# Attention units: three score tiles in flight instead of two, and the last value matmuls between the branch projections

## The reference, cut to what matters

```python
q_a, kc, vc, ks, vs, kw, vw, g_nsa, cq, ckv, kr, g_merge = split(u @ w_in)
# branch a, for each group of 4 heads and each block of 128 queries:
#   three softmaxes (over 15 compressed keys, over the selected keys, over a window), gated and summed
# branch b (latent attention), 8 heads: keys and values from the 256-wide latent, rotary part added
p = exp(s - max(s)); p = p / maximum(sum(p), 1)
y = sigmoid(g_a) * (o_a @ w_branch_a) + sigmoid(g_b) * (o_b @ w_branch_b)
return y @ w_out
```

## Time and profile before

| | |
|---|---|
| runs, median (lowest to highest) | 2415.97 us (2414.37 to 2419.86) |
| profiled execution, its own time | 2425.54 us |
| span of the profiled execution | 2423.5 us |
| mean granted TensorE clock | 0.971 of full |
| PE busy | 2314.7 us, 96% |
| DVE, ACT, POOL busy | 1581.6, 1173.8, 369.3 us |
| attention units of layer 0, of layer 1 | from 331 to 476 us, from 993 to 1138 us |

### The profile page before, as it was taken

The page is one execution under the profiler, slowest core; times in us unless marked ns, Lnnn a source line. Parts: engine busy times, 40 slices in busy tenths (PEclk is TensorE's granted clock), DMA queues, the critical chain, the costliest instruction groups (busy, mean ns, idle before and its releaser), DMA issues.

```text
span 2423.5 us, 41857 instructions
## 1 busy us (share of the span) xinstructions
PE 2314.7 (96%) x17252; PEld 2042.7 (84%) x17252; DVE 1581.6 (65%) x2225; ACT 1173.8 (48%) x2044; POOL 369.3 (15%) x360
## 2 busy tenths in 40 slices
PE   7999999799999999988999999999999998999998
PEld 7888977798888889777888998788878988878887
DVE  5886766578868867665776587267566553535753
ACT  3654444455546544434555566365456411345542
POOL 0110022111101100211111202120132440032001
PEclk9999998899999999988999999999998999999999
DMA  7877742257757766522566554345533300333553
GB/s 267 285 260 239 259 171 97 72 183 267 251 193 280 259 241 251 179 87 87 167 223 210 168 172 143 126 159 189 191 112 122 114 4 3 130 126 115 195 181 105
DMA packets 114236, 417.18 MB, mean 172 GB/s; under 512 B 12672, under 2 KB 12928, under 8 KB 113664
## 3 DMA queue, kind: packets, MB, share of 16 engines
q1 hardware_dynamic: 113184, 409.56, 49.7%
q10 hardware_dynamic: 864, 4.96, 0.5%
HBM read 413.42 MB, written 1.05 MB: 171 GB/s over the span
## 4 chain that ended last, share of the span: by engine, by line
PE 81%; DVE 8%; ACT 4%; issue 4%; POOL 2%; DMA 1%; POOLq 0%; DVEq 0%; ACTq 0%
PE banks L517 80%; DVE weight_lower L1395 2%; ACT heap L2239 1%; DVE weight_ring L1406 1%; POOL heap L2589 1%; ACT weight_upper L2120 1%; PE banks L908 0%; DVE nmax L1552 0%; DVE heap L1550 0%; DVE heap L1533 0%; ACT L2154 0%; DMA weight_ring<-ffn_up_dram 0%; DMA c_rows<-c_rows_dram 0%; PE banks L1196 0%; ACT heap L2284 0%
## 5 line engine op out<-in xcount | busy, mean ns | idle before, releaser
L517 PE MATMUL banks<-xn_halves,weight_upper 128*128 128x512 f32 (+1 forms) x3680 | 1021.0, 349 | 8.0 <-DVE weight_lower L1395 6.0
L1395 DVE TENSOR_TENSOR weight_lower<-weight_ring,weight_upper 128x1024 fp32r<-128x1024 f32 x580 | 738.2, 1279 | 329.2 <-ACT weight_upper L2120 328.0
L517 PE MATMUL banks<-xn_halves,weight_lower 128*128 128x256 f32 x2832 | 809.0, 286 | 23.1 <-DVE branch_a_lower L1587 13.0
L2120 ACT ACTIVATE weight_upper<-weight_ring 128x1024 fp32r<-128x1024 f32 x580 | 608.6, 1054 | 347.7 <-PE banks L517 228.1
L517 PEld LDWEIGHTS banks<-xn_halves,weight_upper 128*128 128x128 f32 x3680 | 650.3, 194 | 99.3 <-DVE weight_lower L1395 6.4
L517 PEld LDWEIGHTS banks<-xn_halves,weight_lower 128*128 128x128 f32 x2832 | 545.5, 193 | 32.3 <-DVE branch_a_lower L1587 15.1
L517 PE MATMUL banks<-hidden,weight_upper 128*128 128x512 f32 x1216 | 428.7, 398 | 4.9 <-DVE heap L1474 4.2
L517 PE MATMUL banks<-hidden,weight_lower 128*128 128x256 f32 x1216 | 340.5, 280 | 0.0
L517 PEld LDWEIGHTS banks<-hidden,weight_upper 128*128 128x128 f32 x1216 | 228.4, 188 | 62.0 <-DVE heap L1474 5.2
L2589 POOL TENSOR_TENSOR heap<-heap 128x256 f32<-128x256 f32 x120 | 121.4, 1016 | 962.6 <-ACT heap L2336 634.9
L517 PEld LDWEIGHTS banks<-hidden,weight_lower 128*128 128x128 f32 x1216 | 229.4, 189 | 0.0
(11 more groups left out here) (287 smaller groups left out, 2610.9 us busy)
## 6 DMA issues: line engine op xcount, KB each, us to landing
weight_ring<-w_ada_dram SPq DMA_DIRECT2D x144, 512.0 KB, 4.4
weight_ring<-ffn_gate_dram SPq DMA_DIRECT2D x88, 512.0 KB, 3.6
weight_ring<-ffn_up_dram SPq DMA_DIRECT2D x88, 512.0 KB, 3.6
weight_ring<-ffn_down_dram SPq DMA_DIRECT2D x88, 512.0 KB, 3.5
weight_ring<-m_w_up_dram SPq DMA_DIRECT2D x64, 512.0 KB, 3.9
weight_ring<-m_w_down_dram SPq DMA_DIRECT2D x64, 512.0 KB, 4.2
weight_ring<-w_in_dram SPq DMA_DIRECT2D x58, 512.0 KB, 4.3
weight_ring<-b_w_rkv_dram SPq DMA_DIRECT2D x24, 512.0 KB, 3.6
```

Of the source, the lines that this page charges most:

```text
L517: return nc.tensor.matmul(o, w, r, start=first, stop=last)
L1395: V.tensor_tensor(w_lo[:, n % RING, :], ring[:, n % RING, :], w_hi[:, j % SPLITS, :].bitcast(F32), ALU.subtract).then_inc(*did("weight_low ...
L2120: A.activation(w_hi[:, j % SPLITS, :], ring[:, n % RING, :], ACT.Copy).then_inc(*did("weight_upper", j))
```

## The change

The scores of unit u lie in place u % 3; the third place is the buffer `latent_n`, whose last reader (the matmuls that make the latent keys, values and queries) stands ahead of the units. `nmax` and `den` get three places too. The banks stay two pairs. PE now computes the scores of units 0 and 1 ahead of the first merge, of unit 2 between merges 1 and 2, and in round u those of unit u+3 instead of u+2. DVE and ACT follow: DVE does `back(u)`, `front(u+3)`, `scale(u+2)` in a round (it was `scale(u+1)`, `back(u)`, `front(u+2)`), ACT does `exps(u+2)` (it was `exps(u+1)`) and then, as before, the merge copy and `back(u)`. The values of the last output run between `w_a` and `w_b` of the first chunk, and their `out_lower` on DVE behind the gating of `w_a`. On ACT the two sigmoids move ahead of the last outputs.

```diff
-        nmax = sb("nmax", [P, 2, HPG])
-        den = sb("den", [P, 2, HPG])
+        nmax = sb("nmax", [P, 3, HPG])
+        den = sb("den", [P, 3, HPG])
+        def scores_of(u):
+            return scores[:, u % 3] if u % 3 < 2 else latent_n[:, 0:HPG, :]
...
-                for m in range(MERGES_FIRST):
-                    merge(m)
                 unit_scores(0)
                 unit_scores(1)
+                merge(0)
+                merge(1)
+                unit_scores(2)
+                for m in range(2, MERGES_FIRST):
+                    merge(m)
...
-                    if u + 2 < NU:
-                        unit_scores(u + 2)
+                    if u + 3 < NU:
+                        unit_scores(u + 3)
...
-                unit_values(todo.pop())
...
+                        if c == 0 and name == "w_b":
+                            unit_values(todo.pop())
...
                 front(0)
                 front(1)
                 scale(0)
+                front(2)
+                scale(1)
                 todo = []
                 for u in range(NU):
-                    if u + 1 < NU:
-                        scale(u + 1)
                     back(u)
+                    if u + 3 < NU:
+                        front(u + 3)
                     if u + 2 < NU:
-                        front(u + 2)
+                        scale(u + 2)
...
-                out_lower(todo.pop())
...
+                        if c == 0 and name == "w_b":
+                            out_lower(todo.pop())
...
-                    if u + 1 < NU:
-                        exps(u + 1)
+                    if u + 2 < NU:
+                        exps(u + 2)
...
+                    if u >= NU - 2:
+                        e = u - (NU - 2)
+                        act.wait_ge(*due("merge", (l, MERGE - 1)))
+                        a = gm[:, e * KD:(e + 1) * KD, :]
+                        A.activation(a, a, ACT.Sigmoid).then_inc(*did("merge_gate", (l, e)))
                 out_t(todo.pop())
-                for e in range(2):
-                    act.wait_ge(*due("merge", (l, MERGE - 1)))
-                    a = gm[:, e * KD:(e + 1) * KD, :]
-                    A.activation(a, a, ACT.Sigmoid).then_inc(*did("merge_gate", (l, e)))
```

More of the change, by code:

```diff
@@ L908, in unit_transpose @@
                             mn = nc.tensor.transpose(bank[0:n, 4 + j // 2, c:c + P],
-                                                     scores[:, u % 2, j, k * P:k * P + n], ident)
+                                                     scores_of(u)[:, j, k * P:k * P + n], ident)
                     mn.then_inc(*did("prob_t_raw", (l, u)))
@@ L1540, in front @@
                     dve.wait_ge(*due("scores_raw", (l, u)))
-                    if u >= 2:
-                        dve.wait_ge(*due("prob_t_raw", (l, u - 2)))
+                    if u >= 3:
+                        dve.wait_ge(*due("prob_t_raw", (l, u - 3)))
                     ps = bank[:, 2 * (u % 2):2 * (u % 2) + 2, :].rearrange("p b (j k) -> p (b j) k", k=S)[:, :, 0:w]
@@ L1548, in front @@
                         bias = const(name).rearrange("p (h k) -> p h k", k=w)[:, g * HPG:(g + 1) * HPG, :]
-                    s_ = scores[:, u % 2, :, 0:w]
+                    s_ = scores_of(u)[:, :, 0:w]
                     V.tensor_tensor(s_, ps, bias, ALU.add).then_inc(*did("biased", (l, u)))
                     dve.wait_ge(*due("biased", (l, u)))
-                    V.tensor_reduce(nmax[:, u % 2, :], s_, AX.X, ALU.max, negate=True).then_inc(
+                    V.tensor_reduce(nmax[:, u % 3, :], s_, AX.X, ALU.max, negate=True).then_inc(
                         *did("row_max", (l, u)))
                     dve.wait_ge(*due("row_max", (l, u)))
-                    V.tensor_scalar(nmax[:, u % 2, :], nmax[:, u % 2, :], MAX_CLAMP, None, ALU.min).then_inc(
+                    V.tensor_scalar(nmax[:, u % 3, :], nmax[:, u % 3, :], MAX_CLAMP, None, ALU.min).then_inc(
                         *did("neg_max", (l, u)))
@@ L1560, in scale @@
                     dve.wait_ge(*due("exps", (l, u)))
-                    d = den[:, u % 2, :]
+                    d = den[:, u % 3, :]
                     V.tensor_scalar(d, d, 1.0, None, ALU.max).then_inc(*did("den", (l, u)))
@@ L2234, in exps @@
                     act.wait_ge(*due("neg_max", (l, u)))
-                    if u >= 2:
-                        act.wait_ge(*due("probs", (l, u - 2)))
+                    if u >= 3:
+                        act.wait_ge(*due("probs", (l, u - 3)))
                     for j in range(HPG):
-                        s_ = scores[:, u % 2, j, 0:w]
-                        A.activation(s_, s_, ACT.Exp, bias=nmax[:, u % 2, j:j + 1],
-                                     accum_out=den[:, u % 2, j:j + 1]).then_inc(
+                        s_ = scores_of(u)[:, j, 0:w]
+                        A.activation(s_, s_, ACT.Exp, bias=nmax[:, u % 3, j:j + 1],
+                                     accum_out=den[:, u % 3, j:j + 1]).then_inc(
                             *did("exp", (l, u, j), also=[("exps", (l, u))] if j == HPG - 1 else []))
@@ L2264, in out_t @@
                         *did("attn_upper", (l, i)))
-                for m in range(MERGES_FIRST):
+                exps(0)
+                merge(0)
+                merge(1)
+                exps(1)
+                for m in range(2, MERGES_FIRST):
                     merge(m)
-                exps(0)
                 todo = []
                 for u in range(NU):
-                    if u + 1 < NU:
-                        exps(u + 1)
+                    if u + 2 < NU:
+                        exps(u + 2)
                     if u + MERGES_FIRST < MERGE:
@@ L2616, in _ @@
                     pool.wait_ge(*of("prob_scale", (l, u)))
-                    s_ = scores[:, u % 2, :, 0:w]
-                    G.tensor_tensor(s_, s_, bcast(den[:, u % 2, :], w), ALU.mult).then_inc(*did("probs", (l, u)))
+                    s_ = scores_of(u)[:, :, 0:w]
+                    G.tensor_tensor(s_, s_, bcast(den[:, u % 3, :], w), ALU.mult).then_inc(*did("probs", (l, u)))
                 sums(3 * l + 2)
```

## The result

The changed kernel ran in 2429.54 us (median of 7, 2423.71 to 2436.58) against 2419.13 us for the kernel before (7 runs, 2414.37 to 2422.57). The ratio is 1.0046, 95% interval 1.0028 to 1.0064: about 11 us slower, and between 7 and 15 by the interval.

A forecast was written before the change was run, and what follows sets the result against it. PE, busy 96% of the span, was taken as the bound. 9.0 - 3.4 + 4.9 - 2.3 + 2.0 - 6.1 = +4.1 us per layer, +8.2 for both, on the 2416.0 median gave 2424.5 us, range 2411 to 2435.

The forecast's parts named there:

- Term A: Start of the units: first scores wait 7.0 us for DVE's last rotary read, plus 2 us clock; +9.0 us per layer.
- Term B: Rounds 0 to 2: the 1.79 us wait of round 2's merge and its half clock go; -3.4 us per layer.
- Term C: Values of outputs 1 and 2: waits for merge copies grow to 3.2 and 3.1 us; +4.9 us per layer.
- Term D: Long wait for `out_lower(2)`: falls from 3.71 to 1.4 us; -2.3 us per layer.
- Term E: Values of output 2: likely to start at half clock after the longer wait; +2.0 us per layer.
- third rival: PE stays at half clock through the values and into the next merges; 8.9 us per layer slower, 2434 us; 15%.
- Term F: End of the units: old waits go, new ones of 0.3, 1.5 and 3.6 us come; -6.1 us per layer.
- the first (the loop does not fall back): Rival: the DVE and ACT loop keeps up at outputs 1 and 2; -2.8 us per layer, 2410 us; 13%.
- the second (the end closes): Rival: no wait from round 12 to `w_a`, some 1.4 us at `w_b`; -2.4 per layer, 2411 us; 12%.
- The fourth: Rival: the third place brings nothing at the end, ACT staying behind `out_t`; +10 us per layer, 2436 us; 4%.

## Why the prediction was right

The forecast was 8.2 us slower, and 10.4 were measured by the medians. (2416.0 + 8.2 is 2424.2, not 2424.5; and the 2.96 us of a merge is the distance between the second and third rows. Neither changes anything.) By its steps:

- **Term A** (+9.0 per layer; 7.0 waiting, 2.0 clock). The wait is 6.69 and 6.84 us. The clock behind it cost 2.9 us, by the run with 28 extra matmuls. Alone it made the kernel 17 us slower (early scores alone), where two times 9.0 were costed.
- **Term B** (-3.4). The wait of 1.79 us in round 2 is gone; one of 0.47 us ahead of a merge came in its place, which was not foreseen. Output 0's wait went from 1.08 to 1.27.
- **Term C** (+4.9; waits of 3.2 and 3.1). They are 3.44 and 3.34 us. That the copy behind the exponentials is the cause was tried: with the copy moved the waits ahead of the values vanish.
- **Term D** (-2.3). 3.71 became 1.40 us, as said.
- **Term E** (+2.0). Output 2's values took 7.15 in place of 5.57 us in layer 0, +1.6, and 10.01 in place of 5.57 in layer 1, +4.4, near the 4.8 of the third rival. The size of this term is not fixed by the wait ahead of it, and that 2 came out near the first layer is luck.
- **Term F** (-6.1; waits of 0.3, 1.5 and 3.6). They are 0.77, 1.58 and 3.86 us, 0.8 more in sum. For the 3.86, ScalarE and VectorE stand as counted: the second sigmoid ends at 469.50, two cuts at 471.39, `out_t(7)` at 472.01, and VectorE's `out_lower` at 474.2.

The waits alone give 25.7 - 20.9 = +4.8 us per layer, where the waits in the forecast's terms (7.0 - 1.8 + 4.9 - 2.3 - 4.8) give +3.0: each step is there, and small misses add up to 1.8. The forecast's other +1.1 is clock. The two stretches show 4.4 and 9.8 us, that is -0.4 and +5.0 besides the waits, so this part can't be called right; that the total came within 2.2 us is in part luck. The mechanism, one new wait at the start, longer waits for copies and shorter ones at the end, was right. Term A's size was right too, but the run with merges first shows that the terms don't simply add: taking A out gave 9 us of the expected 17 to 21, since other waits and the clock took back the rest.

The table load reads 1.28 us again, at 463.40, and the sigmoid starts at 464.69. The drain that the Trainium skill adds to it (ScalarE: Activation LUTs, What ACT_TABLE_LOAD costs) shows in no run here; the wait at `w_b` is within 0.3 us of the sum without it.

Of the rivals, the first (the loop does not fall back) and the second (the end closes) are refuted by the waits. The third (half clock through the values) is partly seen: in layer 1, and in both layers of the run with 28 extra matmuls, output 2 ran at half (10.01 to 10.04 us for its 40 pieces). The fourth falls by Term F's waits.

What I did not see beforehand is that the cause of C stood in the kernel before too: the 4.2 us of copy waits in the earlier trace rows were the key to 32 us, by two calls changed over. What the third place adds to that, with the other repairs in both kernels, is some 4 us that can't be told from zero.

## What to carry to other kernels

Before work is moved forward on an engine, look at which buffers it needs and when their last reader is done: here two scores moved past four merges into banks that another engine held 7 us longer. Where a filler's result has to be evacuated before a bank is used again, the evacuation belongs ahead of the long calls on its engine; here one more buffer in flight did not help while the copy stood last (1.0010 [0.9992, 1.0029] with the start put back). And the price of a wait next to such short matmuls can be more than twice its length, because the granted clock is lower behind it: 6.8 us of waiting removed gave 16 us here.

## What the runs showed of the hardware that I had not expected

The granted clock fell in the value matmuls (64 output columns, partly 15 rows) even with no wait ahead of them, and not in every execution: 0.58 of full in one window and 1.00 in the same window of a kernel with the same order there. The 40 pieces of output 2 took 5.57 us in the kernel before; behind the same wait of 3.34 us they took 7.15 and 10.01 us in the two layers of one execution of the changed kernel. What decides between these is not shown. Where the waits for copies were removed, 6.8 us of waiting per layer were worth 16 us of time, the mean granted clock over the units rising from 0.87 to 0.96.
